# Values of one head at a time, three additions on GpSimd, and split weights for the branch projections

## The chip, the cores and the metric

The kernel runs on one core of one Trainium2 chip. The time is the device time of one execution in microseconds (us). The core has a matrix engine (TensorE, PE in the profile, with its weight loads as PEld), VectorE (DVE), ScalarE (ACT), GpSimd (POOL) and SyncE (SP), which here only issues DMAs. Each engine runs its own list of instructions in order and waits for the others by semaphores.

## What is computed

A network for 256 tokens of width 1024 with 256 context tokens, all in float32. Two trunk layers come first, then a second block. What matters here:

```python
# trunk layer, twice: attention of 8 heads; queries of the context see the context alone
s = jnp.einsum('bqhd,bkhd->bhqk', q, k) * scale        # head width 64 + 32
p = jax.nn.softmax(s, axis=-1)
y = jnp.einsum('bhqk,bkhd->bqhd', p, v)                # value width 64
y = y * jax.nn.silu(z['mla_gate'])
...
x = x + gate * rmsnorm(out, post_g)                    # then the norm of the next layer
# second block
mixed = (g_rwkv * o_rwkv + g_s5 * o_s5) @ w_out        # o_rwkv = y_rwkv @ w_branch_rwkv, o_s5 = y_s5 @ w_branch_s5
x = x + rms_norm(mixed, norm_mix_post)
f = conv_ffn(rms_norm(x, norm_ffn_pre), w_up, conv_w, conv_b, w_down)
x = x + rms_norm(f, norm_ffn_post)
```

The first trunk has queries for all 512 tokens, the second for the 256 of x alone.

## The kernel before

Activations lie turned: 128 features on the partitions, tokens (512, or T = 256) along the free dimension. Weights come from memory as panels of eight 128x128 blocks (512 KB each) into six slots; SyncE issues a panel's load once TensorE has used the panel six before it.

The work is cut into stages that follow each other. At the end of each, `rejoin` makes TensorE, ScalarE and VectorE wait for one another, so the longest engine of a stage sets its length; only the panels' loading and splitting run across the border. Within a stage the order on each engine is the order of the calls in the code.

Two kinds of products exist. Plain ones multiply float32 by float32 (`pe.matmul` at L368; the profile holds two instructions for each such product). Split ones take a weight as hi + lo, both rounded (fp32r), and an operand split likewise, and issue three instructions: hi x hi, hi x lo, lo x hi (L364 to L366). For a split panel ScalarE writes the hi part of the panel (L398, `Rounding.before`) into one of four hi slots, and GpSimd subtracts to get the lo part, half a panel at a time (L408 and L409, `take_rest`). ScalarE's roundings stand at fixed places among its other work, and each may first wait for the panel's load and for TensorE to be done with the panel four splits earlier. GpSimd does nothing else than `take_rest` and belongs to no stage.

Attention: an item is one head and one block of 256 queries. In the first trunk a head has an item for x (512 keys) and one for the context (256 keys); in the second only the one for x. For an item TensorE computes scores (two products, up to 512 columns), VectorE takes the maxima (L885) and negates them (L886), ScalarE takes exponentials and their sums (L865), VectorE divides (L892, L895), TensorE transposes the probabilities (L838) into two banks, ScalarE and VectorE copy one bank each (L875, L903), and TensorE multiplies by the values: for each of four (or two) key tiles a product with 64 weight columns and 256 query columns (issued in L852 to L855, recorded at L368). Two heads make a pair: their value products alternate, head j writing partitions 64j to 64j + 63 of one bank, and VectorE multiplies the whole bank by the gate in one instruction (L910). Steps of three items are in flight.

After a projection's norm, `norm` multiplies o by the inverse root (L685) and adds it to x (L689, L691), eight pieces of 128 x T, all on VectorE; ScalarE squares each piece of x as it comes (L670), and TensorE sums the squares. This happens three times: once with T = 512 (after the first trunk), twice with T = 256.

Second block: `branch_products` multiplies two results, y_s5 and y_rw, by their 1024 x 512 weights: 16 outputs n of 4 products each, all plain. `seq_*` is a chain over four chunks just before it; `out_vector` produces y_rw; `branches_taken` multiplies each output by its gate (L2153) and, from n = 8, adds it to the merged result and splits that (L2156 to L2158).

## Time and profile before

| | us |
|---|---|
| median of three runs (lowest, highest) | 1682.1 (1679.0, 1686.3) |
| the profiled execution, its time | 1686.3 |
| its span in the profile | 1684.5 |
| TensorE busy | 1405.8 (83%) |
| VectorE, GpSimd, ScalarE busy | 843.5, 716.0, 634.8 |
| mean granted TensorE clock | 0.926 of full |

A row of a timeline holds the start from the span's beginning, the length from the first start to the last end, the engine, the line, what is written and read, its size and how many instructions are merged in it; in brackets how long the engine had been idle and who released it. Matrix instructions overlap, so the pace of a series is its length over its count, and the length of a single one is longer than its share. "128*64" means that 64 weight columns were used, "96*128" that 96 rows were.

### The profile page before, as it was taken

The numbers are of one execution on the slowest core, as the hardware profiler recorded it, in microseconds if no ns is written. First come the engines' busy times: TensorE is split into PE (matmuls) and PEld (weight loads), VectorE is DVE, ScalarE is ACT, GpSimd is POOL, SyncE is SP. The second block draws the span as 40 slices with busy tenths as digits, with TensorE's granted clock in tenths as the row PEclk, the third lists the DMA queues.
The fourth block names the chain that finished last, engine by engine and source line by source line (L and its number), as shares of the span: only waits on it lengthen the run. The fifth ranks groups of instructions, "written<-read, shape, count | busy, mean of one in ns | idle before, by whom it ended". The sixth has DMA issues, their size and how long they took to land.

```text
span 1684.5 us, 24559 instructions
## 1 busy us (share of the span) xinstructions
PE 1405.8 (83%) x10288; PEld 1172.8 (70%) x10288; DVE 843.5 (50%) x1205; ACT 634.8 (38%) x987; POOL 716.0 (43%) x512
## 2 busy tenths in 40 slices
PE   5778899899889998578788799957769887699996
PEld 1544588677676876363676789846668776699996
DVE  0437604341423420636765566445979835378801
ACT  2425322343322323425323564635442021455542
POOL 0410044223222643130483767615755003389983
PEclk8889999999999999689998899978889998899998
DMA  8210033144443322120332334513332123256552
GB/s 340 82 53 22 13 100 91 65 162 147 148 151 127 125 88 63 33 82 24 100 113 85 116 108 133 161 48 103 101 111 66 52 64 88 80 181 180 187 165 73
DMA packets 48381, 178.16 MB, mean 106 GB/s; under 512 B 5392, under 2 KB 6416, under 8 KB 47888
## 3 DMA queue, kind: packets, MB, share of 16 engines
q1 hardware_dynamic: 48128, 174.51, 32.6%
q8 instruction: 81, 1.33, 0.3%
q10 hardware_dynamic: 144, 2.10, 0.3%
q14 instruction: 28, 0.23, 0.0%
HBM read 175.54 MB, written 1.05 MB: 105 GB/s over the span
## 4 chain that ended last, share of the span: by engine, by line
PE 60%; DVE 23%; ACT 7%; DMA 3%; issue 3%; POOL 2%; ACTq 1%; DVEq 0%; PEldq 0%; SPq 0%; PEld 0%
PE ps L368 15%; PE ps L364 15%; PE ps L365 14%; PE ps L366 14%; DMA panels<-weights 3%; ACT panels_hi L398 1%; POOL panels_r L409 1%; DVE work L500 1%; POOL panels_r L408 1%; DVE work L1715 1%; PE ps L838 1%; DVE work L951 1%; DVE h_sb L625 1%; DVE work L1169 1%; DVE work L1124 1%
## 5 line engine op out<-in xcount | busy, mean ns | idle before, releaser
L408 POOL TENSOR_TENSOR panels_r<-panels,panels_hi 128x512 fp32r<-128x512 f32 x254 | 369.1, 1453 | 942.4 <-ACT panels_hi L398 941.0
L365 PE MATMUL ps<-h_sb_r,panels_hi 128*128 128x256 f32 (+1 forms) x1408 | 456.1, 324 | 0.0
L398 ACT ACTIVATE panels_hi<-panels 128x1024 fp32r<-128x1024 f32 x254 | 267.4, 1057 | 437.4 <-PE ps L366 263.4
L409 POOL TENSOR_TENSOR panels_r<-panels,panels_hi 128x512 fp32r<-128x512 f32 x254 | 360.2, 1418 | 0.0
L364 PE MATMUL ps<-hi_sb_r,panels_hi 128*128 128x512 f32 (+1 forms) x784 | 280.9, 358 | 47.3 <-DVEq L2368 24.5
L365 PEld LDWEIGHTS ps<-h_sb_r,panels_hi 128*128 128x128 f32 x1408 | 280.0, 199 | 17.4 <-issue 0.8
L366 PE MATMUL ps<-hi_sb_r,panels_r 128*128 128x512 f32 (+1 forms) x784 | 274.3, 350 | 0.0
L364 PE MATMUL ps<-h_sb_r,panels_hi 128*128 128x256 f32 x624 | 184.3, 295 | 39.5 <-DVEq L2368 17.6
L364 PEld LDWEIGHTS ps<-hi_sb_r,panels_hi 128*128 128x128 f32 x784 | 154.8, 197 | 75.9 <-DVEq L2368 26.5
L364 PE MATMUL ps<-work_r,panels_hi 128*128 128x256 f32 (+1 forms) x560 | 179.9, 321 | 24.8 <-DVEq L2368 13.8
L366 PE MATMUL ps<-h_sb_r,panels_r 128*128 128x256 f32 x624 | 180.9, 290 | 0.0
L365 PE MATMUL ps<-work_r,panels_hi 128*128 128x256 f32 (+1 forms) x560 | 178.5, 319 | 0.0
L366 PE MATMUL ps<-work_r,panels_r 128*128 128x256 f32 (+1 forms) x560 | 177.9, 318 | 0.0
L366 PEld LDWEIGHTS ps<-hi_sb_r,panels_r 128*128 128x128 f32 x784 | 154.6, 197 | 18.0
L364 PEld LDWEIGHTS ps<-h_sb_r,panels_hi 128*128 128x128 f32 x624 | 124.7, 200 | 43.2 <-DVEq L2368 18.4
L500 DVE RECIPROCAL work<-work 128x256 f32<-128x256 f32 (+3 forms) x6 | 20.1, 3353 | 237.9 <-ACTq L2368 237.9
L364 PEld LDWEIGHTS ps<-work_r,panels_hi 128*128 128x128 f32 x560 | 108.9, 194 | 35.7 <-DVEq L2368 15.0
L368 PE MATMUL ps<-work 64*64 64x64 f32 (+6 forms) x1488 | 113.0, 278 | 23.4 <-DVE work L1279 6.1
L366 PEld LDWEIGHTS ps<-h_sb_r,panels_r 128*128 128x128 f32 x624 | 124.6, 200 | 0.0
L368 PE MATMUL ps<-work,panels 128*128 128x256 f32 (+2 forms) x288 | 93.2, 483 | 33.6 <-DVEq L2368 22.1
L366 PEld LDWEIGHTS ps<-work_r,panels_r 128*128 128x128 f32 x560 | 109.3, 195 | 6.6
L365 PEld LDWEIGHTS ps<-work_r,panels_hi 128*128 128x128 f32 x560 | 109.0, 195 | 6.2
(310 smaller groups left out, 1864.7 us busy)
## 6 DMA issues: line engine op xcount, KB each, us to landing
panels<-weights SPq DMA_DIRECT2D x323, 512.0 KB, 3.6
x_sb<-x_in SPq DMA_DIRECT2D x1, 2048.0 KB, 8.2
x_sb<-x_in ACTq DMA_DIRECT2D x1, 2048.0 KB, 11.4
const_sb<-constants SPq DMA_DIRECT2D x1, 1216.0 KB, 10.7
out<-x_sb SPq DMA_DIRECT2D x1, 1024.0 KB, 4.8
vec_sb<-vectors SPq DMA_DIRECT2D x1, 725.0 KB, 12.0
small<-c_in SPq DMA_DIRECT2D x1, 8.0 KB, 1.8
```

Source lines behind the costliest of these rows:

```text
L364: pe.matmul(o, lhsT.hi, rhs.hi, start=start, stop=False)
L365: pe.matmul(o, lhsT.hi, rhs.lo, start=False, stop=False)
L366: mm = pe.matmul(o, lhsT.lo, rhs.hi, start=False, stop=stop)
L368: mm = pe.matmul(o, lhsT, rhs, start=start, stop=stop)
L398: act.activation(panels_hi[:, m:m + PANEL * P], panels[:, n:n + PANEL * P], ACT.Copy).then_inc(panel_rounded, 1)
L408: pool.tensor_tensor(panels_r[:, at:at + half], panels[:, at:at + half], panels_hi[:, m:m + half], ALU.subtract)
L409: pool.tensor_tensor(panels_r[:, at + half:at + 2 * half], panels[:, at + half:at + 2 * half], panels_hi[:, m + half:m + 2 * half], ALU.su ...
L500: steps["dve"](dve.reciprocal(inverse[:, 0:at[-1]], root[:, 0:at[-1]]))
L625: ins = dve.scalar_tensor_tensor(h[:, m, t0:t0 + n], x[:, m, t0:t0 + n], gains[l][:, m, c:c + 1], inverse[:, t0:t0 + n], ALU.mult, ALU.mult)
L838: mm = pe.transpose(ps[:, 4 + kt // (nkt // 2), (kt % (nkt // 2)) * 256 + t * P: (kt % (nkt // 2)) * 256 + (t + 1) * P], probs[j % 3][:, t ...
L951: step(dve.tensor_tensor(dst[:, :, lo:hi], src[:, :, lo - back:hi - back], src[:, :, lo + ahead:hi + ahead], ALU.add))
L1124: dve.tensor_tensor(merged[:, m, :], merged[:, m, :], dst, ALU.add).then_inc(added, 1)
```

## The change

Three edits stand together.

**Attention.** Items go head by head instead of pair by pair; the value products of an item are issued as soon as that item's transposes are copied, all into one half of a bank, and the gate multiply becomes one of 64 partitions for each item. The two value buffers alternate (two copies of `probs_t` instead of four).

**Additions to x.** The first three of the eight additions (pieces 5, 6, 7) go to GpSimd; VectorE keeps all eight multiplies and five additions. GpSimd's part becomes part of the stage's end.

**Branch weights.** The eight panels of the two branch weights are split panels now, so their 64 products become 192 instructions. y_s5 and y_rw are split too: one rounding copy of 128x1024 on ScalarE (`y5_round`, `yr_round`) and one subtraction of 128x1024 on VectorE (`y5_rest`, `yr_rest`) each.

```diff
@@ stream_plan
-        add(f"branch_{name}", tiles_of(f"w_branch_{name}_2", 0, 512, 0, D))
+        add(f"branch_{name}", tiles_of(f"w_branch_{name}_2", 0, 512, 0, D), split=True)
@@ norm, ScalarE
-                        act.wait_ge(by_dve, d0 + i + 1)
+                        if i < 3:
+                            act.wait_ge(by_pool, p0 + i + 1)
+                        else:
+                            act.wait_ge(by_dve, d0 + i - 2)
@@ norm, VectorE
-                        if i:
+                        if i >= 4:
                             j = order[i - 1]
                             dve.wait_ge(times, t0 + i)
                             dve.tensor_tensor(x[:, j, :], x[:, j, :], o[:, j, :], ALU.add).then_inc(by_dve, 1)
@@ norm, GpSimd
+            def gpsimd(pool):
+                for i, m in enumerate(order[:3]):
+                    pool.wait_ge(times, t0 + i + 1)
+                    pool.tensor_tensor(x[:, m, :], x[:, m, :], add[0][:, m, :], ALU.add).then_inc(by_pool, 1)
+                    pool.wait_ge(by_pool, p0 + i + 1)
@@ attention
-            items = [(hd + j, q0, 0 if q0 == 0 else SEQ) for hd in range(0, HEADS, 2) for q0 in range(0, TQ, SEQ) for j in range(2)]
+            items = [(hd, q0, 0 if q0 == 0 else SEQ) for hd in range(HEADS) for q0 in range(0, TQ, SEQ)]
@@ attention, TensorE
-                    if i >= 3 and i % 2 == 0:
-                        n = (i - 3) // 2
-                        hd, q0, k0 = items[2 * n]
...
-                        for kt in range(nkt):
-                            for j in range(2):
-                                blocks.product(pe, ps[VDIM * j:VDIM * j + VDIM, 6 + n % 2, 0:256],
-                                               v_t[:, k0 // P + kt, (hd + j) * VDIM:(hd + j + 1) * VDIM],
-                                               probs_t[(2 * n + j) % 4][:, kt, :], kt == 0, kt == nkt - 1,
-                                               valued if kt == nkt - 1 and j else None)
+                    if i >= 3:
+                        j = i - 3
+                        hd, q0, k0 = items[j]
+                        nkt, r0 = (TOK - k0) // P, VDIM * (hd % 2)
+                        pe.wait_ge(turned_act, i0 + j + 1)
+                        pe.wait_ge(turned_dve, i0 + j + 1)
+                        if j >= 2:
+                            pe.wait_ge(gated, i0 + j - 1)
                         for kt in range(nkt):
+                            blocks.product(pe, ps[r0:r0 + VDIM, 6 + j % 2, 0:256],
+                                           v_t[:, k0 // P + kt, hd * VDIM:(hd + 1) * VDIM], probs_t[j % 2][:, kt, :],
+                                           kt == 0, kt == nkt - 1, valued if kt == nkt - 1 else None)
@@ attention, VectorE
-                        y = y_mla[:, hd // 2, q0:q0 + 256]
-                        dve.tensor_tensor(y, ps[:, 6 + n % 2, 0:256], y, ALU.mult).then_inc(gated, 1)
+                        y = y_mla[r0:r0 + VDIM, hd // 2, q0:q0 + 256]
+                        dve.tensor_tensor(y, ps[r0:r0 + VDIM, 6 + j % 2, 0:256], y, ALU.mult).then_inc(gated, 1)
@@ second block
+            def y5_round(act):
+                act.wait_ge(y5_ready, 1)
+                act.activation(parts_s5.hi, y_s5, ACT.Copy).then_inc(y5_rounded, 1)
+            def y5_rest(dve):
+                dve.wait_ge(y5_rounded, 1)
+                dve.tensor_tensor(parts_s5.lo, y_s5, parts_s5.hi, ALU.subtract).then_inc(y5_split, 1)
...
+            def yr_round(act):
+                act.wait_ge(out_done, 2)
+                act.activation(parts_rw.hi, y_rw, ACT.Copy).then_inc(yr_rounded, 1)
+            def yr_rest(dve):
+                dve.wait_ge(yr_rounded, 1)
+                dve.tensor_tensor(parts_rw.lo, y_rw, parts_rw.hi, ALU.subtract).then_inc(yr_split, 1)
@@ branch_products
                     if n == 0:
-                        pe.wait_ge(y5_ready, 1)
+                        pe.wait_ge(y5_split, 1)
                     if n == KD:
-                        pe.wait_ge(out_done, 2)
+                        pe.wait_ge(yr_split, 1)
@@ scalar
                 seq_scalar(act, 2)
+                y5_round(act)
                 seq_scalar(act, 3)
...
                 branch_rounding(act, 4, KD)
+                yr_round(act)
                 branch_rounding(act, KD, 2 * KD)
@@ vector
                 seq_vector(dve, 2)
+                y5_rest(dve)
                 seq_vector(dve, 3)
...
                 out_vector(dve)
+                yr_rest(dve)
                 branches_taken(dve, KD, 2 * KD)
```

TensorE in the first trunk's attention, before (512-column score products are those of an item with 512 keys, 128x128 ones the transposes, 64x256 ones the value products):

```order
L368 MATMUL ps<-work 128x512 x2
L838 MATMUL ps<-const_sb,work 128x128 x4
L368 MATMUL ps<-work 64x256 x8
L368 MATMUL ps<-work 128x512 x2
L838 MATMUL ps<-const_sb,work 128x128 x4
L368 MATMUL ps<-work 128x256 x2
L838 MATMUL ps<-const_sb,work 128x128 x8
L368 MATMUL ps<-work 64x256 x4
```

The same place in the changed kernel:

```order
L368 MATMUL ps<-work 128x512 x2
L846 MATMUL ps<-const_sb,work 128x128 x8
L368 MATMUL ps<-work 64x256 x2
L368 MATMUL ps<-work 128x256 x2
L846 MATMUL ps<-const_sb,work 128x128 x4
L368 MATMUL ps<-work 64x256 x4
```

A run of eight value products for two heads has become a run of four for one head, and runs of four have become runs of two; there are 16 runs where there were 8. The number of products is the same.

VectorE in the norm after the first trunk, before:

```order
L685 TENSOR_TENSOR work<-work 128x512 x2
L689 TENSOR_TENSOR x_sb<-x_sb,work 128x512
L685 TENSOR_TENSOR work<-work 128x512
L689 TENSOR_TENSOR x_sb<-x_sb,work 128x512
L685 TENSOR_TENSOR work<-work 128x512
```

and in the changed kernel:

```order
L688 TENSOR_TENSOR work<-work 128x512 x5
L692 TENSOR_TENSOR x_sb<-x_sb,work 128x512
L688 TENSOR_TENSOR work<-work 128x512
L692 TENSOR_TENSOR x_sb<-x_sb,work 128x512
```

Five multiplies stand ahead of the first addition. GpSimd has, between two panels' subtractions, the three additions:

```order
L409 TENSOR_TENSOR panels_r<-panels,panels_hi 128x512
L709 TENSOR_TENSOR x_sb<-x_sb,work 128x512 x3
L408 TENSOR_TENSOR panels_r<-panels,panels_hi 128x512
```

ScalarE around the branch products, in the changed kernel (L2083 and L2085 are the last chunks of the chain, L1776 and L2128 the new roundings of y_s5 and y_rw, L398 the roundings of panels):

```order
L1776 ACTIVATE work_r<-work 128x1024
L2083 ACTIVATE work<-ps 128x256
L2085 ACTIVATE work<-ps 128x4x64
L398 ACTIVATE panels_hi<-panels 128x1024
L2104 ACT_TABLE_LOAD
L2104 ACTIVATE small<-small 128x16
L398 ACTIVATE panels_hi<-panels 128x1024 x2
L2128 ACTIVATE work_r<-work 128x1024
```

Before, no L398 row stood between the last chunk and the table load (four in a row came after it), and the two roundings of y did not exist.

## Rows read from the trace of the kernel before

**Rows 1.** The page: busy time by engine; the chain that ended last, by engine.

```profile
PE 1405.8 (83%) x10288; PEld 1172.8 (70%) x10288; DVE 843.5 (50%) x1205; ACT 634.8 (38%) x987; POOL 716.0 (43%) x512
...
PE 60%; DVE 23%; ACT 7%; DMA 3%; issue 3%; POOL 2%; ACTq 1%; DVEq 0%; PEldq 0%; SPq 0%; PEld 0%
```

**Rows 2.** TensorE in time, first trunk's attention: start, length, instructions, [idle, releaser].

```profile
157.15 3.86 PE L368 MATMUL ps<-work 128*64 128x256 f32 x20
...
161.29 1.03 PE L368 MATMUL ps<-work 96*128 96x256 f32 x4
164.34 1.06 PE L838 MATMUL ps<-const_sb,work 128*128 128x128 f32 x8 [2.02 <-ACT work L875]
165.33 2.15 PE L368 MATMUL ps<-work 128*64 128x256 f32 x12
...
170.61 3.86 PE L368 MATMUL ps<-work 128*64 128x256 f32 x20
```

**Rows 3.** TensorE in time, second trunk's attention.

```profile
791.09 3.86 PE L368 MATMUL ps<-work 128*64 128x256 f32 x20
...
799.48 3.86 PE L368 MATMUL ps<-work 128*64 128x256 f32 x20
...
807.87 1.95 PE L368 MATMUL ps<-work 128*64 128x256 f32 x16
```

**Rows 4.** TensorE in time: products of 64 columns, all into one half.

```profile
134.76 1.88 PE L368 MATMUL ps<-work,panels 128*64 128x512 f32 x4
```

**Rows 5.** VectorE and ScalarE in time, first trunk's attention.

```profile
161.05 1.23 DVE L885 TENSOR_REDUCE small<-ps 128x2 f32<-128x1024 f32 x1 [1.45 <-PE ps L368]
...
162.51 0.69 ACT L865 ACTIVATE work<-ps,small 128x512 f32<-128x512 f32 x1 [2.68 <-DVE small L886]
...
165.68 0.60 ACT L875 ACTIVATE work<-ps 128x512 f32<-128x512 f32 x1
```

**Rows 6.** VectorE in time, additions to x: 512 tokens, then 256.

```profile
673.92 1.29 DVE L685 TENSOR_TENSOR work<-work 128x512 f32<-128x512 f32 x2
...
682.96 0.68 DVE L691 TENSOR_TENSOR x_sb<-x_sb,work 128x512 f32<-128x512 f32 x1
...
1454.58 0.76 DVE L685 TENSOR_TENSOR work<-work 128x256 f32<-128x256 f32 x2
...
1459.62 0.41 DVE L691 TENSOR_TENSOR x_sb<-x_sb,work 128x256 f32<-128x256 f32 x1
```

**Rows 7.** VectorE and GpSimd in time, second block.

```profile
1413.35 1.51 POOL L408 TENSOR_TENSOR panels_r<-panels,panels_hi 128x512 fp32r<-128x512 f32 x1 [4.18 <-ACT panels_hi L398]
1413.77 1.25 DVE L2157 CAST work_r<-work 128x256 fp32r<-128x256 f32 x1
...
1415.05 1.38 DVE L2158 TENSOR_TENSOR work_r<-work,work_r 128x256 fp32r<-128x256 f32 x1
```

**Rows 8.** TensorE in time, the branch products.

```profile
1383.99 8.90 PE L368 MATMUL ps<-work,panels 128*128 128x256 f32 x40 [0.67 <-DVE work L2153]
...
1400.52 16.88 PE L368 MATMUL ps<-work,panels 128*128 128x256 f32 x64 [5.62 <-DVE work L2106]
```

**Rows 9.** VectorE in time, around the branch products.

```profile
1374.68 0.42 DVE L2050 COPY work<-ps 128x256 f32<-128x256 f32 x1 [1.33 <-PE ps L368]
...
1395.05 1.39 DVE L2105 TENSOR_TENSOR work<-work 128x512 f32<-128x512 f32 x1
1396.47 1.63 DVE L2106 TENSOR_TENSOR work<-work,hi_sb 128x512 f32<-128x512 f32 x1
...
1399.77 0.69 DVE L2106 TENSOR_TENSOR work<-work,hi_sb 128x512 f32<-128x512 f32 x1
1404.34 0.42 DVE L2153 TENSOR_TENSOR work<-ps,work 128x256 f32<-128x256 f32 x1 [3.87 <-PE ps L368]
```

**Rows 10.** TensorE in time, split products that follow each other.

```profile
1080.02 0.28 PE L365 MATMUL ps<-work_r,panels_hi 128*128 128x256 f32 x1
...
1080.14 0.28 PE L366 MATMUL ps<-work_r,panels_r 128*128 128x256 f32 x1
```

More of the change, by code:

```diff
@@ L648, in norm @@
             (times, t0) = shared("o_times", KD * added)
-            (by_dve, d0) = shared("x_dve_added", KD * added)
+            (by_pool, p0), (by_dve, d0) = shared("x_pool_added", 3 * added), shared("x_dve_added", 5 * added)
             (squared, q0), (summed, s0), (rooted, r0) = shared("x_squared", KD), shared("x_summed", 1), shared("x_rooted", 1)
@@ L701, in vector @@
                         scale[2](dve, m - 1, h, split.hi, split.lo).then_inc(split_done, 1)
-            return Stage(tensor, scalar, vector, None), (split_done, l0)
+            def gpsimd(pool):
[3 more added lines that the diff above has]
+                    pool.wait_ge(by_pool, p0 + i + 1)
+            return Stage(tensor, scalar, vector, gpsimd if add is not None else None), (split_done, l0)
         def residual(name, block0, rhs, T, gain_cols, at, last_x=None, aside={}):
@@ L807, in trunk @@
             probs = [room(2, TOK) for _ in range(3)]
-            probs_t = [room(4, 256) for _ in range(4)]
+            probs_t = [room(4, 256) for _ in range(2)]
             top, total, share = [region(small, 300 + 6 * i, 3, 2) for i in range(3)]
-            items = [(hd + j, q0, 0 if q0 == 0 else SEQ) for hd in range(0, HEADS, 2) for q0 in range(0, TQ, SEQ) for j in range(2)]
+            items = [(hd, q0, 0 if q0 == 0 else SEQ) for hd in range(HEADS) for q0 in range(0, TQ, SEQ)]
             n_items = len(items)
@@ L872, in attn_scalar @@
                         act.wait_ge(turned, i0 + j + 1)
-                        if j >= 4:
-                            act.wait_ge(valued, p0 + j // 2 - 1)
-                        act.activation(probs_t[j % 4][:, 0:half, :],
+                        if j >= 2:
+                            act.wait_ge(valued, i0 + j - 1)
+                        act.activation(probs_t[j % 2][:, 0:half, :],
                                        ps[:, 4, 0:half * 256].rearrange("p (k q) -> p k q", q=256),
@@ L900, in attn_vector @@
                         dve.wait_ge(turned, i0 + j + 1)
-                        if j >= 4:
-                            dve.wait_ge(valued, p0 + j // 2 - 1)
-                        dve.tensor_copy(probs_t[j % 4][:, half:2 * half, :],
+                        if j >= 2:
+                            dve.wait_ge(valued, i0 + j - 1)
+                        dve.tensor_copy(probs_t[j % 2][:, half:2 * half, :],
                                         ps[:, 5, 0:half * 256].rearrange("p (k q) -> p k q", q=256)).then_inc(turned_dve, 1)
-                    if i >= 3 and i % 2 == 0:
-                        n = (i - 3) // 2
-                        hd, q0, _ = items[2 * n]
-                        y = y_mla[:, hd // 2, q0:q0 + 256]
-                        dve.wait_ge(valued, p0 + n + 1)
-                        dve.tensor_tensor(y, ps[:, 6 + n % 2, 0:256], y, ALU.mult).then_inc(gated, 1)
+                    if i >= 3:
+                        j = i - 3
+                        hd, q0, _ = items[j]
+                        r0 = VDIM * (hd % 2)
+                        y = y_mla[r0:r0 + VDIM, hd // 2, q0:q0 + 256]
+                        dve.wait_ge(valued, i0 + j + 1)
+                        dve.tensor_tensor(y, ps[r0:r0 + VDIM, 6 + j % 2, 0:256], y, ALU.mult).then_inc(gated, 1)
             stages.append(Stage(attn_tensor, attn_scalar, attn_vector, None))
```

16 lines of the change are left out of this document (7 added, 9 removed).

## The prediction

> **What bounds the kernel now.** I read the page first: TensorE is busy for 83% of the span and carries 60% of the chain that ended last, VectorE 23% [rows 1]. No engine is full and stages end together, so each edit is priced in its own stage, from the timelines of the engines that wait there: attention (157 us and 791 us), the three additions to x (674, 1110 and 1454 us), the branch products (1374 to 1423 us). A gain elsewhere would not carry over the stage's end.
>
> In attention TensorE is nearly the bound. In the first trunk the same row comes back after 13.46 us (157.15 to 170.61), that is for two heads, and TensorE is idle for only 2.02 us of it, ahead of the transposes of an item with 512 keys [rows 2]. In the second trunk the period for two heads is 8.39 us [rows 3].
>
> **Attention: value products alone in their half.** What does a value product cost? The clean row has eight of them for two heads (16 instructions) in 1.95 us [rows 3], 0.24 us each. Four instructions of 64 columns by 512 that all write one half took 1.88 us, 0.47 each [rows 4]; half that width is then 0.235 us an instruction and 0.47 a product. So the alternating halves ran side by side, two for the price of one, and products that follow each other in one half do not. A run of four for one head thus lasts as long as the run of eight for two did: 1.93 us; a run of two lasts what four did: 2.15 less the 256-wide scores that the row also holds, about 1.05 us [rows 2]. There are 16 such runs where there were 8 in the first trunk, and 8 where there were 4 in the second.
>
> Walk one head of the first trunk in the new order, from the scores of the item with 512 keys. TensorE: those scores 1.85 us (a row of 3.86 less a value run), transposes of the item before 0.95, its neighbour's values 1.05, 256-wide scores 0.93. Meanwhile the scored item passes VectorE (1.23 and the small negation, 1.46), ScalarE's two exponentials with their sums (two of 0.67, 1.34) and ScalarE's copy of the transposed bank, 0.56 [rows 5]; only then, at 3.36 plus three handovers of 0.05, may the next transposes write. That is 3.51 + 1.85 = 5.36 us after the scores began, while TensorE's own list is through at 4.78: it waits 0.58. Then transposes 0.50 and the long values 1.93. Sum 4.78 + 0.58 + 2.43 = 7.79 us for a head, 15.58 for two against 13.46. Four pairs of heads: +8.5 us. The same walk with the old order gives 13.3 where the trace has 13.46, so it can be trusted to some 0.2 us a pair.
>
> Second trunk: an item is 1.85 + 0.95 + 1.93 = 4.73 us on TensorE alone, which no longer waits; two are 9.46 against 8.39, +1.07 for each of the four pairs, +4.3. The first pair starts through an empty pipeline that waits in either kernel, so I take +4.0. The twelve extra gate multiplies of VectorE (0.4 us each) lie in its waits. Bounds: were every added TensorE microsecond on the path, 8 x (1.93 + 1.05) / 2 = 11.9 and 4 x 1.93 = 7.7, +19.6; were the switch into and out of a run free, some 0.2 less a run, 9.3. I take +12.5.
>
> **Additions on GpSimd.** VectorE's chain of eight multiplies and eight additions runs from 673.92 to 683.64 for 512 tokens and from 1454.58 to 1460.03 for 256: 0.61 and 0.34 us a piece [rows 6]. ScalarE's squares and the sum follow the last addition, so the chain is on the path. Three pieces fewer would give back 1.8, 1.0 and 1.0. But the two engines do not run side by side here. Where GpSimd subtracts panels, a VectorE rounding of 256 columns takes 1.25 us and a subtraction 1.38, and each ends just after GpSimd's instruction does (1413.35 + 1.51 = 1414.86, VectorE's ends at 1415.02) [rows 7]: it sits until GpSimd is through, and GpSimd's next one stretches in turn. In the norm every instruction of both engines reads two operands from SBUF, so the pieces add up: VectorE 13 x 0.61 = 7.9, GpSimd 3 x 1.25 (it hands over at that pace: 512 columns in 1.27 to 1.51) = 3.75, together 11.7 against 9.7: +1.9. For 256 tokens the trace has no GpSimd instruction; bounds are half of 1.25 and 1.25 itself. At 0.65, near the half since the work is by element: 13 x 0.34 + 3 x 0.65 = 6.35 against 5.45, +0.9, twice. Sum +3.7; the ends are -3.8 (side by side) and +7.3.
>
> The Trainium skill says the same of the cause: in "SBUF — State Buffer", section "SBUF: two separate sides", the port pair of the two engines is an exclusive lock, which a VectorE instruction with two SBUF inputs takes as well as GpSimd's. By this rule the edit costs time, and rows 7 agree. "GPSIMD Engine Reference", section "Elementwise — side-by-side cycle accounting", has 2.6 cycles an element at 1.2 GHz, an estimate of 0.55 us and an overhead for 256 columns; no run here shows it yet, and by it the 256-token norms would cost much what I took.
>
> **Branch products.** Split weights cost three instructions that follow each other at 0.12 us (1080.02, 1080.14) [rows 10], 0.36 a product, where 20 plain ones took 8.90 us, 0.44 each [rows 8]. The 64 products would save 5 us if TensorE were the bound; mostly it isn't. In order of time:
> - Three extra roundings stand before the last gates, one before the glu; ScalarE and GpSimd are idle there, and what VectorE waits for is TensorE. Nothing. If that cover fails, a subtraction of a panel costs VectorE about 1.3.
> - y5_rest (1.2 us) waits for ScalarE until about 1374.3 and stands in front of the chain's next copy, due at 1374.68 [rows 9]: +0.8 on the chain.
> - The 20 products after the first three outputs take 7.2 instead of 8.9; with the +0.8, out_tensor comes 0.8 us earlier.
> - A panel's subtraction no longer falls on out_vector (GpSimd would be done with the third by 1394): its additions of 1.39 and 1.63 go back to 0.69 each [rows 9]: -1.6. y_rw is ready 2.4 earlier.
> - yr_round (1.06) and yr_rest (1.2) follow, all on the path: +2.3. TensorE starts the second half where it did, at 1400.4.
> - There the first output took 3.87 us, at half the pace of the rest [rows 8, 9]; twelve instructions at twice 0.12 are 2.9, -0.9. From then VectorE is the bound (L2153 to L2158, 1.58 us an output when alone, 12.6 for eight) plus about 1.5 for each panel subtracted meanwhile: three before, three and a little more now. -1.0.
>
> Sum -2.0, with ends of -5 (TensorE's whole saving) and +5 (five panels' subtractions beside VectorE, nothing saved in out_vector, the roundings exposed).
>
> **Sum.** +12.5 + 3.7 - 2.0 = +14.2 us. The profiled execution would go from a span of 1684.5 to 1698.7 (time 1700.5). It was the slowest of three, 4.2 above their median of 1682.1; against the median the forecast is 1696.3.
>
> **Rivals.**
> - *VectorE and GpSimd overlap after all.* Then the additions give 3.8 us: 12.5 - 3.8 - 2.0 = +6.7, 1688.8. Against it are rows 7; for it, that GpSimd there subtracts long panels. Chance 0.12.
> - *Half-wide products cost half (not slower).* If a 64-column product in one half ran at 0.24 us alone, a run for one head would be half as long, items would leave the pipeline one step sooner, and my walk gives +1.4 in the first trunk and -2.6 in the second: total -1.2 + 3.7 - 2.0 = +0.5, 1682.6. It decides at a long value run of about 1.0 us. For it: rows 4 have 512 columns and other data. Chance 0.06.
> - *The saved TensorE time is not hidden and its clock gains.* TensorE waits less in attention (0.58 twice for 2.02), so fewer stretches at low clock: branch -5 and attention -4 against the sum give +7, 1689. Chance 0.08.
> - *The split exposes the branch*: its upper end of +5 instead of -2, 1703. Chance 0.14.
> - The forecast: 0.60.
>
> A difference of 0.5%, 8.4 us, is about what a measurement of this kernel tells from no change. The forecast (0.60) and the exposed branch (0.14) are slower, and so is a part of the third rival, 0.04: 0.78. The first two rivals and the rest of the third are within 0.5%, but for 0.03 in which two of them meet and it is faster: 0.19. The range, 1687 to 1704, holds the forecast with its bounds and most of the rivals at either side.
>
> **What would show it.** Right: value rows of x8 (four products) at 1.9 us and a period of about 15.6 us for two heads in the first trunk, 9.5 in the second; additions to x that take 11.7 and 6.3 us, with VectorE instructions of 1.3 us or more beside GpSimd's; out_vector without long additions; y_rw split between 1398 and 1401 on this trace's clock. Wrong: value rows of x8 near 1.0 us; VectorE's pieces of 0.34 and 0.61 unchanged while GpSimd adds; TensorE waiting in the branch for panel_split. The time itself would be wrong if the stretches at low clock shift by more than a few us, which no edit controls.

## The result, and the profile after

The changed kernel takes 1689.16 us (median of 6 runs, 1688.38 to 1690.32), the kernel before 1680.8 (6 runs, 1674.2 to 1686.32): a ratio of 1.0051, 95% interval 1.0033 to 1.0069. It is slower by 8.4 us; the forecast was +14.2, to 1696.3. The profiled execution has a span of 1691.7 us against 1684.5, +7.2, at nearly the same mean clock (0.927, 0.926).

Page of the changed kernel, engines and chain, against [rows 1]:

```profile
PE 1415.7 (84%) x10352; PEld 1178.7 (70%) x10352; DVE 854.5 (51%) x1210; ACT 644.5 (38%) x997; POOL 745.7 (44%) x537
...
PE 59%; DVE 24%; ACT 7%; DMA 4%; issue 3%; POOL 3%; ACTq 1%; DVEq 0%; PEldq 0%; SPq 0%; PEld 0%; POOLq 0%
```

TensorE gained 10 us of busy time though the branch's products became cheaper, and GpSimd 30 us: 16 half panels and nine additions.

**Attention.** TensorE in the first trunk, against [rows 2] (L846 are the transposes; a row of x12 holds a head's eight value instructions and the next scores, the x8 at 203.30 the values alone):

```profile
163.01 0.63 PE L846 MATMUL ps<-const_sb,work 128*128 128x128 f32 x4 [0.59 <-ACT work L881]
163.57 3.85 PE L368 MATMUL ps<-work 128*64 128x256 f32 x12
167.26 1.04 PE L846 MATMUL ps<-const_sb,work 128*128 128x128 f32 x8
168.23 2.14 PE L368 MATMUL ps<-work 128*64 128x256 f32 x8
170.96 0.63 PE L846 MATMUL ps<-const_sb,work 128*128 128x128 f32 x4 [0.59 <-ACT work L881]
171.51 3.85 PE L368 MATMUL ps<-work 128*64 128x256 f32 x12
...
203.30 1.94 PE L368 MATMUL ps<-work 128*64 128x256 f32 x8
```

A head comes back after 7.94 us (163.57 to 171.51), two after 15.9, where two took 13.46. The wait is 0.59 a head, and four products for one head take 1.94 us (203.30), as eight for two heads did [rows 3]. From the first maxima to the last gate multiply the stage lasts 67.60 us instead of 58.51: +9.1. In the second trunk:

```profile
790.68 3.86 PE L368 MATMUL ps<-work 128*64 128x256 f32 x12
794.37 1.04 PE L846 MATMUL ps<-const_sb,work 128*128 128x128 f32 x8
795.34 3.85 PE L368 MATMUL ps<-work 128*64 128x256 f32 x12
```

4.66 us an item, 9.32 for two against 8.39 [rows 3]; the stage takes 41.57 us for 39.30: +2.3.

**Additions to x.** VectorE and GpSimd, 512 tokens, then 256, against [rows 6]:

```profile
677.90 6.30 DVE L688 TENSOR_TENSOR work<-work 128x512 f32<-128x512 f32 x5
678.74 4.92 POOL L709 TENSOR_TENSOR x_sb<-x_sb,work 128x512 f32<-128x512 f32 x3 [15.59 <-DVE work L688]
...
680.39 1.60 POOL L709 TENSOR_TENSOR x_sb<-x_sb,work 128x512 f32<-128x512 f32 x1
680.79 1.75 DVE L688 TENSOR_TENSOR work<-work 128x512 f32<-128x512 f32 x1
...
684.13 0.68 DVE L692 TENSOR_TENSOR x_sb<-x_sb,work 128x512 f32<-128x512 f32 x1
...
1461.31 3.35 DVE L688 TENSOR_TENSOR work<-work 128x256 f32<-128x256 f32 x5
1461.88 2.50 POOL L709 TENSOR_TENSOR x_sb<-x_sb,work 128x256 f32<-128x256 f32 x3 [6.26 <-DVE work L688]
```

The rows at 680.39 and 680.79 are the second addition and the fourth multiply, taken out of their series. The first two multiplies start 0.61 us apart, as before; the three that have a GpSimd addition beside them start 1.67 apart and last 1.75 each (0.87 and 0.94 for 256 tokens). Once GpSimd is done, VectorE's instructions are 0.61 apart again. The chains last 11.12, 6.03 and 6.03 us instead of 9.72, 5.45 and 5.45. But what follows them did not move as much: from the first multiply to the reciprocal of the norm it is +0.4, 0.0 and +0.6 us. The reason is TensorE's series of 16 instructions that sums the squares; here in the norm of 1110 us, first before, with the granted clock during the chain and behind it, then after:

```profile
1112.07 5.67 PE L368 MATMUL ps<-work,const_sb 128*128 128x256 f32 x16 [5.59 <-ACT work L670]
...
1110.32:1116.08 5.76, 4.01 (x10) 3.24 (x11) 5.45 (x16) 3.11 (x8) 0.00 (x0) 0.50 0.01 1
1116.08:1118.30 2.22, 1.66 (x8) 1.12 (x6) 0.02 (x1) 0.61 (x2) 0.00 (x0) 1.00 0.00 0
```
```profile
1116.27 5.44 PE L368 MATMUL ps<-work,const_sb 128*128 128x256 f32 x16 [5.83 <-ACT work L673]
```

It starts 1.75 us after the first multiply before and 1.99 after. TensorE had been idle for 5.6 us ahead of it, and the granted clock is 0.50, the lower of its two levels (1.2 GHz), until 1116.08 us: there the instructions are 0.43 us apart, behind it 0.22, as plain products of that size are at full clock [rows 8]. So the series, which runs without a gap to its end in both kernels, sets the end there and not the last addition. In the first norm, where the chain is 1.4 us longer, the last products wait for squares, and 0.4 us are left of it. Of the third norm's +0.6 the clock has a part: it is 0.61 over that stretch in the changed kernel and 0.78 before. With the attention edit alone (e1, clock 0.61) the same stretch takes 8.30 us without any addition moved, and with the additions alone (e2, 0.79) 8.18, against 7.96 before and 8.53 here: the moved additions cost 0.2 of it.

**Branch.** VectorE and ScalarE, against [rows 9]:

```profile
1380.40 1.22 DVE L1780 TENSOR_TENSOR work_r<-work,work_r 128x1024 fp32r<-128x1024 f32 x1 [0.86 <-ACT work_r L1776]
1381.54 0.42 DVE L2068 COPY work<-ps 128x256 f32<-128x256 f32 x1
...
1401.12 0.69 DVE L2124 TENSOR_TENSOR work<-work,hi_sb 128x512 f32<-128x512 f32 x1
...
1404.20 1.06 ACT L2128 ACTIVATE work_r<-work 128x1024 fp32r<-128x1024 f32 x1 [7.30 <-DVE work L2124]
1405.29 1.23 DVE L2132 TENSOR_TENSOR work_r<-work,work_r 128x1024 fp32r<-128x1024 f32 x1 [1.12 <-ACT work_r L2128]
1409.54 0.42 DVE L2179 TENSOR_TENSOR work<-ps,work 128x256 f32<-128x256 f32 x1 [3.02 <-PE ps L366]
```

As forecast, y5_rest stands in front of the chain's last copy (+0.7), `out_vector` has no long additions, y_rw is ready 2.4 us earlier on the stage's clock, its rounding and subtraction take 2.3 back, and VectorE waits 3.02 us for the first output of the second half, not 3.87. Then GpSimd's subtractions fall beside VectorE's split:

```profile
1412.78 1.35 POOL L408 TENSOR_TENSOR panels_r<-panels,panels_hi 128x512 fp32r<-128x512 f32 x1 [1.21 <-ACT panels_hi L398]
1414.09 1.34 POOL L409 TENSOR_TENSOR panels_r<-panels,panels_hi 128x512 fp32r<-128x512 f32 x1
1413.02 1.26 DVE L2183 CAST work_r<-work 128x256 fp32r<-128x256 f32 x1
1414.31 1.40 DVE L2184 TENSOR_TENSOR work_r<-work,work_r 128x256 fp32r<-128x256 f32 x1
```

Beside these outputs four panels are subtracted, before three, and seven of VectorE's instructions last 1.13 to 1.40 us there, before five (1.04 to 1.38). A wait of 1.1 us for TensorE ahead of the second output is gone. From the first to the last output the second half takes 19.3 us, before 18.4. The stage is 0.1 us shorter than before, not 2.0.

**What is left.** The stages that the change touches sum to 9.1 + 2.3 + 1.0 - 0.1 = +12.3 us in these two traces, yet the spans differ by 7.2. The other 5.1 us came back in stages whose code is the same: 1.7 before the attention begins, 3.4 between it and the norm of its trunk (466.74 us, then 463.36), 2.7 around the second trunk, while 2.2 were lost ahead of the branch's chain and 0.7 behind the branch. Two windows of before, then three of the changed kernel (busy of PE, PEld, DVE, ACT, POOL; granted clock; DMA):

```profile
300.00:350.00 50.00, 45.94 (x180) 33.85 (x178) 20.45 (x20) 18.40 (x18) 10.14 (x8) 0.97 0.26 85
500.00:550.00 50.00, 46.65 (x245) 35.40 (x245) 16.13 (x24) 14.38 (x17) 15.10 (x12) 0.93 0.46 168
```
```profile
300.00:350.00 50.00, 44.79 (x180) 33.17 (x179) 19.79 (x22) 19.91 (x20) 13.29 (x10) 1.00 0.26 85
500.00:550.00 50.00, 45.87 (x249) 34.39 (x247) 16.12 (x24) 14.53 (x17) 15.60 (x12) 0.97 0.52 194
...
1341.70:1348.50 6.80, 6.02 (x116) 5.83 (x112) 6.69 (x9) 0.67 (x2) 0.00 (x0) 0.50 0.01 2
```

In the first two the granted clock of TensorE is 0.97 and 0.93 before, 1.00 and 0.97 after. They are those that differ most; over the whole stretch between the attention and the norm it is 0.97 before and 0.98 after. The third is where the 2.2 us were lost: a stretch of 6.8 us at the lower level (0.50), which the trace of before does not have; up to there this part of the two kernels runs alike to 0.2 us. Whether the edits did that is a question for experiments.

### The profile page after: what moved, and what is told of

It is laid out like the page before. It is cut to its first block, busy times and chain, and to the rows that moved or that the text cites. A ratio compares the mean times of both kernels' runs of the same rounds, so it can differ in the third digit from the quotient of the medians.

```text
span 1691.7 us, 24769 instructions
## 1 busy us (share of the span) xinstructions
PE 1415.7 (84%) x10352; PEld 1178.7 (70%) x10352; DVE 854.5 (51%) x1210; ACT 644.5 (38%) x997; POOL 745.7 (44%) x537
## 4 chain that ended last, share of the span: by engine, by line
PE 59%; DVE 24%; ACT 7%; DMA 4%; issue 3%; POOL 3%; ACTq 1%; DVEq 0%; PEldq 0%; SPq 0%; PEld 0%; POOLq 0%
PE ps L364 15%; PE ps L366 14%; PE ps L365 14%; PE ps L368 14%; DMA panels<-weights 3%; ACT panels_hi L398 1%; POOL panels_r L409 1%; DVE work L500 1%; POOL panels_r L408 1%; DVE work L1725 1%; DVE h_sb L625 1%; DVE work L958 1%; DVE work L1176 1%; DVE work L1131 1%; PE ps L846 1%
## 5 line engine op out<-in xcount | busy, mean ns | idle before, releaser
L408 POOL TENSOR_TENSOR panels_r<-panels,panels_hi 128x512 fp32r<-128x512 f32 x262 | 378.4, 1444 | 888.6 <-ACT panels_hi L398 886.8
L398 ACT ACTIVATE panels_hi<-panels 128x1024 fp32r<-128x1024 f32 x262 | 275.9, 1057 | 455.2 <-PE ps L366 291.0
L409 POOL TENSOR_TENSOR panels_r<-panels,panels_hi 128x512 fp32r<-128x512 f32 x262 | 371.3, 1417 | 0.0
L364 PE MATMUL ps<-work_r,panels_hi 128*128 128x256 f32 (+1 forms) x624 | 199.2, 319 | 35.7 <-DVEq L2398 14.6
L366 PE MATMUL ps<-work_r,panels_r 128*128 128x256 f32 (+1 forms) x624 | 197.1, 316 | 0.0
L365 PE MATMUL ps<-work_r,panels_hi 128*128 128x256 f32 (+1 forms) x624 | 196.9, 316 | 0.0
L364 PEld LDWEIGHTS ps<-work_r,panels_hi 128*128 128x128 f32 x624 | 122.1, 196 | 47.3 <-DVEq L2398 15.6
L364 PEld LDWEIGHTS ps<-h_sb_r,panels_hi 128*128 128x128 f32 x624 | 124.6, 200 | 43.2 <-DVEq L2398 18.4
L368 PE MATMUL ps<-work 64*64 64x64 f32 (+6 forms) x1488 | 132.8, 279 | 22.5 <-ACT work L871 6.2
L365 PEld LDWEIGHTS ps<-work_r,panels_hi 128*128 128x128 f32 x624 | 122.0, 195 | 6.2
L366 PEld LDWEIGHTS ps<-work_r,panels_r 128*128 128x128 f32 x624 | 121.6, 195 | 6.6
L368 PEld LDWEIGHTS ps<-work 64*64 64x64 f32 (+4 forms) x1488 | 82.4, 146 | 60.8 <-issue 24.3
## 6 DMA issues: line engine op xcount, KB each, us to landing
const_sb<-constants SPq DMA_DIRECT2D x1, 1216.0 KB, 10.6
```

The source lines that it names most:

```text
L364: pe.matmul(o, lhsT.hi, rhs.hi, start=start, stop=False)
L365: pe.matmul(o, lhsT.hi, rhs.lo, start=False, stop=False)
L366: mm = pe.matmul(o, lhsT.lo, rhs.hi, start=False, stop=stop)
L368: mm = pe.matmul(o, lhsT, rhs, start=start, stop=stop)
L398: act.activation(panels_hi[:, m:m + PANEL * P], panels[:, n:n + PANEL * P], ACT.Copy).then_inc(panel_rounded, 1)
L408: pool.tensor_tensor(panels_r[:, at:at + half], panels[:, at:at + half], panels_hi[:, m:m + half], ALU.subtract)
```

## Experiments

Two yardsticks are used beside the median. *By stage*: the same stretch in two traces, since most stretches whose code is the same agree to some 0.3 us where the clock falls alike (some do not: the untouched branch stage took 73.7 to 74.1 us in the traces of before and five experiments, and 72.6 in e5's). *At equal clock*: each execution lists its span and its mean granted clock. Those of before range from 1669.6 us at 0.936 to 1682.3 at 0.926; over 59 of them the span falls by 9.3 us for each 0.01 of clock (correlation -0.88). The distance of a kernel's executions from that line says what it costs at the same clock. Two limits: a single execution of before scatters about the line by 1.4 us, and the profiled one (1684.5 at 0.926) lies 5 us above it; and if an edit itself changes the clock, this yardstick leaves that part out.

| kernel | median, before | ratio, 95% | at equal clock |
|---|---|---|---|
| changed kernel (15 executions) | 1689.2, 1680.8 | 1.0051, 1.0033 to 1.0069 | +11.9 ± 0.3 |
| e1 attention alone | 1687.2, 1678.8 | 1.0038, 1.0023 to 1.0053 | +10.9 ± 0.3 |
| e2 additions alone | 1679.0, 1678.8 | 1.0004, 0.9987 to 1.0021 | +1.9 ± 0.8 |
| e3 branch alone | 1676.2, 1678.8 | 0.9981, 0.9967 to 0.9995 | -1.8 ± 0.6 |
| e4 values head after head | 1689.2, 1678.8 | 1.0044, 1.003 to 1.0058 | +8.7 ± 0.7 |
| e5 all additions on GpSimd | 1684.3, 1678.6 | 1.0045, 1.003 to 1.0061 | +5.0 ± 0.8 |
| e6 branch, fitted | 1673.8, 1678.6 | 0.9973, 0.9959 to 0.9986 | -2.9 ± 0.5 |
| e7 groups of two | 1685.5, 1678.6 | 1.0041, 1.0026 to 1.0055 | +3.0 ± 0.1 |
| e8 values later | 1670.6, 1678.6 | 0.9955, 0.9943 to 0.9967 | -9.1 ± 0.4 |
| e9 values later, branch fitted | 1666.7, 1677.7 | 0.9931, 0.9911 to 0.995 | -11.0 ± 0.4 |
| e10 only y_s5's weight split | 1676.1, 1677.7 | 0.9988, 0.9973 to 1.0002 | -3.1 ± 0.4 |
| e11 values later and e10 | 1666.1, 1677.7 | 0.993, 0.9909 to 0.9951 | -13.9 ± 0.7 |

(± is one standard error over the kernel's own executions; the line's own is 0.2. For e7, with four executions, the ± of 0.1 is chance: by the line's scatter of 1.4 it is 0.7.)

**The three edits apart** (e1 to e3: the kernel before with the attention hunks, the norm hunks and the branch hunks of the change).

> The kernel before with the attention edit alone. In the changed kernel the two attention stages lasted 9.1 and 2.3 us longer, yet the whole only 8.4 us (medians), since stages whose code is the same came out shorter. Theory A (the value products cost what the walk says, and later unchanged stages give some of it back because stretches at low clock are gone there): attention of the first trunk +9 us, of the second +2.3 us (value rows of x8 at 1.94 us), and the whole +6 to +9 us. Theory B (what is given back belongs to run-to-run scatter, not to this edit): the whole +11 to +12 us. Theory C (half-wide products are not slower when alone; the longer stage came from something else in the changed kernel): under +2 us.

> The kernel before with the three additions of each norm on GpSimd alone. Theory A (VectorE and GpSimd take turns, the chain is 1.4, 0.6 and 0.6 us longer, but TensorE's tail behind it gives part back): the whole +0.5 to +2 us, VectorE multiplies beside GpSimd 1.26 us apart instead of 0.61 for 512 tokens and 0.67 instead of 0.34 for 256. Theory B (my forecast): +3.7 us. Theory C (the two engines overlap): -3.8 us.

> The kernel before with split branch weights alone. Theory A (from the changed kernel's trace: y_rw comes 2.4 us earlier, its rounding and subtraction take 2.3 back, the second half lasts 0.9 us longer since GpSimd's subtractions of four panels fall beside VectorE's split): the stretch from the chain's first copy to the last split output -0.1 us, the whole -1 to +1 us. Theory B (the roundings of the new panels also delay what stands ahead of the branch, +2.2 us in the stretch before the chain at a low clock): the whole +2 to +3 us. Theory C (my forecast): -2 us.

By stage, e1 has the changed kernel's attention to 0.15 us (67.60 and 41.44), e2 its additions (11.12, 6.03, 6.03), e3 its branch (-0.3; changed kernel -0.1). At equal clock the three sum to 10.9 + 1.9 - 1.8 = 11.0 against 11.9 ± 0.3, which is within the errors of the three: the edits add up, and nearly all of the loss is attention. The stretch between the first trunk's attention and its norm, whose code is the same in all, took 463.1 us in e1, 466.9 in e2, 460.9 in e3, and 460.7 to 467.6 in the others. So the 3.4 us that "came back" there are within what this stretch scatters by in any kernel, and the profiled execution of before lay at its long end. Of e1's theories the traces (+11.2) and the equal clock (+10.9) speak for B, the median (+8.4) for A, and the two can't be told apart: e1's seven executions have a mean clock of 0.9309, the 24 of before beside them 0.9282, a difference of 0.0027 with a standard error of 0.0009, and 2.5 us by the line. Whether the longer attention raises the clock elsewhere stays open; against it is that the changed kernel, with the same attention, has 0.9296 over 15 executions, where the 59 of before have 0.9288. Theory A of e2 holds (the forecast's 3.7 doesn't). e3 is split: its stage (-0.3) is theory A's, its whole, -2.5 us by the median and -1.8 ± 0.6 at equal clock, lies outside A's -1 to +1 and nearer to my forecast's -2. The 2.2 us that the changed kernel's trace lost ahead of the chain are in none of the other twelve, though e3's roundings stand at the same places: the low stretch at 1341.7 us, which made them, is in its trace alone. What decides where the low stretches fall was not found.

**Why single-head runs cost double.** e4 and e7 keep the pairs and change only the order of the products within one.

```diff
-                        for kt in range(nkt):
-                            for j in range(2):          # before: j alternates
+                        for j in range(2):              # e4: one head, then the other
+                            for kt in range(nkt):
+                        (e7: two kt of one head, two of the other, and again)
```

> The kernel before, and only the order of the value products within a pair changed: first the four (or two) of one head, then those of the other, instead of alternating between the halves. Items, buffers, gate multiplies and counts are those of before. Theory A (alternating halves run side by side, two for the price of one; in a row in one half they don't): the row of 16 instructions takes 3.9 us instead of 1.95; the first trunk's attention gains 4 x (1.93 + 1.05) = 11.9 us less the waits of TensorE that this fills (up to 2.0 a pair), +4 to +12 us; the second's at most 4 x 1.93 = 7.7 us, +4 to +8. Theory B (a half-wide product costs the same in any order, and the changed kernel's longer attention comes from head-by-head items and the doubled number of runs): rows of 16 stay at 1.95 us, the whole within 1 us of before.

> The kernel before with the value products of a pair in groups of two products (four instructions) per head: two of one head, two of the other, and again. Four per head at a time took 2.85 us for 16 instructions where alternating took 1.95, and one head alone 1.94 for eight. Theory A (the two halves run side by side as soon as the order reaches the other one, up to about four instructions ahead): groups of two products lose little, 1.95 to 2.3 us for 16 instructions, the whole within 1.5 us of before. Theory B (only direct neighbours overlap, and each change of half gives a fixed 0.1 to 0.3 us back): 16 instructions take 3.8 less three changes, 2.9 us or more, the whole +5 us or more.

TensorE in e4, then in e7; a row of x20 holds 16 instructions of values and the next item's scores (four instructions, 1.88 us):

```profile
796.20 4.78 PE L368 MATMUL ps<-work 128*64 128x256 f32 x20
...
811.84 2.83 PE L368 MATMUL ps<-work 128*64 128x256 f32 x16 [0.83 <-ACT work L875]
```
```profile
795.80 3.91 PE L368 MATMUL ps<-work 128*64 128x256 f32 x20
...
804.24 2.00 PE L368 MATMUL ps<-work 128*64 128x256 f32 x16
```

Sixteen instructions take 1.95 us alternating [rows 3], 2.00 in groups of four (two products), 2.83 in groups of eight, and a single head's eight 1.94. So the halves do run side by side, and the order needs to reach the other half within about four instructions. e4's trace shows it by the starts of the single instructions in its last row (811.84): four start one by one, 0.22 us apart, then four times two together, by the order of issue one of each half, then four one by one. So the second head's first instruction starts beside the fifth of the first head's eight. A head alone pays the full price: its instructions start 0.22 us apart (1.94 us for eight), like those of products over all 128 columns [rows 8]. e4's stages lose 3.8 and 5.4 us; theory A holds, but for 2.83 us a row and not 3.9, since it had no overlap at all, and 3.8 is just below its range. (Of the 5.4 us 1.6 are the clock's lower level: one row of 16 took 3.95 us and the transposes ahead of it 1.58 instead of 1.06, and both overlap a stretch of 3.4 us with a granted clock of 0.50.) The Trainium skill, "TensorEngine Tiling (Array Packing)", section "When to Use Tiling", gives 2x column tiling for 64 columns. The trace agrees with 1.95 us for 16 against 1.94 for eight, and adds that the order decides. The rival that half-wide products cost half is out: the changed kernel's price comes from having nothing in the other half beside a head's products. e7's stages are those of before but for 0.5 and 0.3 us (58.98 and 39.61), as its theory A has it, and its rows rule out theory B's 2.9 us. Yet its whole is not within A's 1.5 us: the median is 7 us higher. The mean clock is 0.925, 0.0038 below that of the 18 executions beside it (standard error 0.0009), which is 3.5 us of it by the line, and +3.0 at equal clock is left. Whether the order of the products lowers the clock or these four executions did, and where the 3.0 us are, stays open.

**Are VectorE and GpSimd exclusive?** e5 gives GpSimd all eight additions of a norm.

> The kernel before with all eight additions of each norm on GpSimd; VectorE keeps the eight multiplies. Theory A (VectorE and GpSimd take turns; one GpSimd addition adds 1.64 - 0.61 = 1.03 us for 512 tokens and 0.83 - 0.34 = 0.49 us for 256): the chain takes 8 x (0.61 + 1.03) = 13.1 us instead of 9.7, and 8 x (0.34 + 0.49) = 6.6 instead of 5.45; the whole +3.4 + 1.2 + 1.2 = +5.8 us at most, +4 with the tail behind it. Theory B (they overlap, and GpSimd's pieces are simply slower): 8 x 1.03 + 0.61 = 8.9 us and 8 x 0.49 + 0.34 = 4.3, the whole -0.8 - 1.2 - 1.2 = -3.2 us.

```profile
668.66 11.32 DVE L685 TENSOR_TENSOR work<-work 128x512 f32<-128x512 f32 x8
669.50 12.94 POOL L700 TENSOR_TENSOR x_sb<-x_sb,work 128x512 f32<-128x512 f32 x8 [15.59 <-DVE work L685]
```

Eight multiplies take 11.32 us, GpSimd's eight additions 12.94. The chain is 13.78 us (forecast 13.1; side by side would be 8.9) and 7.34 for 256 tokens. Theory A: the engines take turns. Less eight multiplies, an addition adds 1.11 us (13.78 - 8 x 0.61 = 8.9), and 0.58 for 256 tokens; the 1.03 expected took 4.92 us over three additions for their distance, while they start 1.67 apart. The last addition, which has no multiply beside it, takes 1.26 us. Part is again hidden by the sum of squares: to the reciprocal it is +2.8, +1.1 and +1.1 us, and the median says +5.7.

**Does the walk hold?** If the wait of 2.02 us is set by scores, maxima, exponentials and a copy, work put inside it is free. e8 moves a pair's value products there, and the gate multiply with them.

```diff
 for i in range(n_items + 3):
     scores(i)
+    if i >= 5 and i % 2 == 1 and i <= n_items + 1:
+        values(pe, (i - 5) // 2)
     transposes(i - 2)
-    if i >= 3 and i % 2 == 0:
-        values(pe, (i - 3) // 2)
+    if i == n_items + 2:
+        values(pe, n_items // 2 - 1)
```

> The kernel before, pairs and alternating value products kept; a pair's value products and its gate multiply stand one step later, between the next item's scores and the transposes, where TensorE waits 2.0 us a pair in the first trunk and 0.94 in the second. Theory A (the walk of the forecast holds: the wait runs from an item's scores over maxima, exponentials and copy, 5.36 us, and any work of TensorE put inside it is free): the first trunk's period per pair goes from 13.46 to about 11.6 us, the second's from 8.39 to 7.6, the whole -6 to -10 us. Theory B (VectorE, busy 10.4 us a pair, or the later gate multiply becomes the bound): -1 to -4 us. Theory C (TensorE, waiting less, gains or loses nothing, for another wait takes its place): within 1 us.

```profile
156.90 3.76 PE L368 MATMUL ps<-work 96*128 96x512 f32 x20
160.59 0.66 PE L854 MATMUL ps<-const_sb,work 128*128 128x128 f32 x4
161.09 1.03 PE L368 MATMUL ps<-work 96*128 96x256 f32 x4
162.37 1.07 PE L854 MATMUL ps<-const_sb,work 128*128 128x128 f32 x8 [0.25 <-DVE work L915]
...
168.33 3.76 PE L368 MATMUL ps<-work 96*128 96x512 f32 x20
```

The wait ahead of the long item's transposes has shrunk from 2.02 to 0.25 us, and a pair takes 11.43 us, later 11.60 (forecast 11.6); in the second trunk 7.21 (forecast 7.6). What is waited for now is VectorE's copy (L915). The stages are 7.5 and 2.6 us shorter, the kernel 8.0 us faster. Theory A. (In e11 the first stage is 51.05 us, in e9 52.44 with the same code, so a single trace is good to some 1.4 us here.)

**The branch, fitted.**

```diff
                 seq_vector(dve, 2)
-                y5_rest(dve)
                 seq_vector(dve, 3)
+                y5_rest(dve)
 ...            yr_round, yr_rest:
+                for g in range(2): two = slice(2 * g, 2 * g + 2)    # after out_done g + 1
```

> Split branch weights alone, placed otherwise: y5_rest stands behind the chain's last copy, where VectorE waits 3.3 us for ScalarE, instead of ahead of it; y_rw is rounded and subtracted in two halves, the first while VectorE makes the second, and TensorE's first products wait for the first half only. Theory A (both steps were exposed, as the forecast had it): the chain's last copy comes 0.7 us earlier than with the branch edit alone, y_rw is split 1.1 us earlier after it is ready, the first output of the second half 1.1 to 1.7 us earlier; the stretch from the chain's first copy to the last split output -2 to -2.5 us against before (it was -0.3 with the branch edit alone). Theory B (GpSimd's subtractions set the pace in the second half, through the lock with VectorE and the panels' order): the second half starts earlier and ends where it did, the stretch -0.3 to -1 us.

> The fitted branch, but only the weight of y_s5 is split; the second half of the branch (y_rw) keeps plain products, so y_rw is neither rounded nor subtracted and four panels fewer are split. Theory A (the first half carries the gain: fewer panel subtractions beside out_vector and shorter products give 3.2 us until y_rw is ready, and the second half is bound by VectorE and GpSimd, not by TensorE): y_rw ready 3 us earlier than before on the stage's clock, the second half 22.3 us as before or up to 1.5 us shorter since no new subtractions fall beside VectorE's split; the stage -3 to -4.5 us. Theory B (the split of the second half is worth its cost): the second half is 0.5 us or more longer than with the fitted branch, the stage -2.5 us or less.

```profile
1372.97 0.42 DVE L2061 COPY work<-ps 128x256 f32<-128x256 f32 x1 [1.33 <-PE ps L368]
1373.31 1.22 DVE L1773 TENSOR_TENSOR work_r<-work,work_r 128x1024 fp32r<-128x1024 f32 x1
...
1395.51 1.47 DVE L2129 TENSOR_TENSOR work_r<-work,work_r 128x512 fp32r<-128x512 f32 x2
1399.23 0.42 DVE L2177 TENSOR_TENSOR work<-ps,work 128x256 f32<-128x256 f32 x1 [2.25 <-PE ps L366]
```

In e6 the copy comes first and y5_rest costs nothing; y_rw's subtractions begin where the last multiply ends. From the chain's first copy to the last output the stage takes 71.00 us (before 74.14, e3 73.84): -3.1, more than forecast; both steps had been exposed. e10 comes to 70.10, 49.69 until y_rw is ready (e6: 48.69) and 20.41 behind it (e6: 22.31, before 22.26), and the same branch in e11 to 71.56, since there GpSimd's subtractions fell on `out_vector` (additions of 1.73 and 1.63 us). By its median e10 is not told apart from before (ratio 0.9988, up to 1.0002). So the second weight's split earns about what it costs, as theory A says; which of the two branches is better by under 1 us the runs don't tell.

**Together.** e9 is e8 with e6, e11 is e8 with e10.

> The kernel before with the value products one step later in attention and the fitted split branch (y5_rest behind the chain's last copy, y_rw split in halves) together. By stages of the two apart: -7.5 and -2.6 us in attention, -3.1 us in the branch. Theory A (the parts add up, as the three of the changed kernel did): the whole -11 to -14 us, about 1666 us where before is 1678.6. Theory B (TensorE, waiting less, gets a lower granted clock later and gives much of it back): -7 to -9 us.

> The value products one step later and the branch with only the weight of y_s5 split, together. If the parts add up: -7.5 - 2.6 in attention and what that branch alone gives (forecast -3 to -4.5), the whole -12 to -15 us; otherwise, if the granted clock takes some back, -8 to -10 us.

1666.7 and 1666.1 us, 11.0 and 11.6 below before: the two can't be told apart, and both beat it by 0.7%. By stage e9 has e8's attention (52.44 and 36.67 us; 50.97 and 36.68 in e8) and e6's branch (71.05). At equal clock 9.1 + 2.9 = 12.0 stand against 11.0, and 9.1 + 3.1 = 12.2 against 13.9: the parts add up within the scatter, as theory A of e9 has it. The medians lie at the near edge of what was expected (-11 to -14) and just short of it (-12 to -15).

## Why the prediction was right, and where its sizes were off

- *The base.* The forecast's 1696.3 rests on 1682.1, a median of three. Over 59 executions before is at 1678.6; against that the changed kernel is at +10.6, and at equal clock +11.9. The time came out 7 us below the forecast's, and two rivals (1688.8 and 1689) lie closer to the measured 1689.2 than the forecast does. That it lies in the range is in part luck with the base and the clock; what bears the forecast out are the stages, +12.3 by trace for +14.2.
- *Half-wide products, the period of the first trunk*: right. 1.94 us for a head's run, 15.9 us for two heads where the walk had 15.58, +9.1 for +8.5. (The lower bound of 9.3 took 0.2 us off sixteen runs; the edit adds twelve, eight and four, which gives 10.1. Nothing else rests on it.) e4 and e7 show the cause, e8 that the walk's wait is real.
- *Second trunk*: +2.3 for +4.0. The period was right (9.32 for 9.46). But I charged four pairs with it, and only two whole periods follow each other: from the first pair's values to the third's 16.78 us before (791.09 to 807.87), 18.64 after (790.68 to 809.32), +1.9. The rest is the pipeline's filling and its tail, where the fourth pair came 3.81 us after the third and TensorE waits in either order; they cost 0.4.
- *Additions on GpSimd*: right that the engines take turns (e2, e5), wrong in two sizes. A piece on GpSimd adds 1.06 us for 512 columns in the changed kernel (11.12 - 13 x 0.61 = 3.19 for three) and 1.11 in e5, not 1.25 (I took the price of subtractions that write a rounded type), and 0.54 and 0.58 for 256, not 0.65. By the Trainium skill's "GPSIMD Engine Reference", section "Elementwise — side-by-side cycle accounting", an estimate for 256 columns is 0.55 us; the trace agrees, with 0.54 to 0.58 on top of VectorE's piece. And "the chain is on the path" failed: the chains are 2.6 us longer in sum (1.40, 0.58, 0.58), but what sets the norm's end in the 256-token norms is TensorE's series of squares at the clock's lower level, which starts 0.24 us later. +1.0 for +3.7, and about 0.35 of the 1.0 is the clock in the third norm.
- *Branch*: each step up to the second half's first output came as worked out (+0.7, -1.5, -1.6, +2.3, -0.9). The last term failed: +0.9 for -1.0. I had taken the second half as bound by VectorE with little more than three panels beside it; four were subtracted there, and seven of VectorE's instructions were long where before had five. -0.1 for -2.0 by trace; e3's executions say -1.8 ± 0.6 at equal clock, so how far this term was off is not settled.
- *The rivals.* Overlap of the engines is refuted by e5, half price by the 1.94 us of a head's run. "The clock gains" fits the number (+7) but not by its sum: it wanted 4 us less in attention and -5 in the branch, and these stages came to +11.4 and -0.1. That the clock gives something back outside them is neither shown nor excluded (e1). The exposed branch did not happen, but two of its steps were exposed, and e6 took them away.

## What to carry to other kernels

Products that use half of TensorE's columns were cheap here only while something ran in the other half: keep pairs together, and fill an engine's wait by moving work inside the loop before reordering the loop. Before an edit moves work from VectorE to GpSimd, look whether both read two operands from SBUF at that moment; here the pieces then added up. When a stage seems to end with one engine's chain, check that the series behind it isn't as slow. Judge edits below 1% by stage and at equal clock beside the median, which moved by 3.5 us by itself here (1682.1 for three executions, 1678.6 for 59), and look whether the edit's own executions have another clock, which the equal-clock figure hides.

## What the runs showed of the hardware

- 64-column products of 256 columns: 16 instructions in 1.95 us alternating between halves, 2.00 in groups of four, 2.83 in groups of eight; eight alone 1.94.
- The starts in e4: with eight instructions of one half ahead of eight of the other, the other half's first starts beside the fifth of the first half's.
- A GpSimd addition and a VectorE multiply, both with two operands in SBUF: pairs start 1.67 us apart for 128x512 (VectorE alone 0.61) and 0.87 for 128x256 (alone 0.34); over eight pairs the chain is 13.78 and 7.34 us.
- The series of squares: 0.43 us an instruction at a granted clock of 0.50, 0.22 at full clock.
- The 59 executions of before differ by up to 12.7 us in span (1669.6 to 1682.3), and the mean granted clock (0.936, 0.926) goes with it.
